# Swapping the two 48 KB weight regions between gate and up in an expert loop on one Trainium2 core

## The reference, cut to what matters

```python
def swiglu(h, wg, wu, wd):
    return (jax.nn.silu(h @ wg) * (h @ wu)) @ wd

def moe_swiglu(h, w_router, wg, wu, wd):
    logits = (t @ w_router).astype(jnp.float32)
    top_vals, top_idx = lax.top_k(logits, TOP_K)
    ...
    def expert(acc, xs):
        g_e, wg_e, wu_e, wd_e = xs
        return acc + g_e[:, None].astype(t.dtype) * swiglu(t, wg_e, wu_e, wd_e), None
```

## Time and profile before

| what | us |
|---|---|
| median of 3 runs (1561.59 to 1564.09) | 1562.27 |
| the profiled execution, its device time | 1563.21 |
| its span from the first to the last instruction | 1561.4 |
| start of item 0 on PE | about 643 |
| end of item 0 (big) on PE | 755.5 |
| end of item 1 (small) on PE | 858.6 |
| end of item 7 on PE | 1513.7 |

### The profile page before, as it was taken

The page is one execution under the profiler, slowest core; times in us unless marked ns, Lnnn a source line. Parts: engine busy times, 40 slices in busy tenths (PEclk is TensorE's granted clock), DMA queues, the critical chain, the costliest instruction groups (busy, mean ns, idle before and its releaser), DMA issues.

```text
span 1561.4 us, 26124 instructions
## 1 busy us (share of the span) xinstructions
PE 1453.6 (93%) x11620; PEld 854.2 (55%) x11620; DVE 486.5 (31%) x619; ACT 392.1 (25%) x457; POOL 73.1 (5%) x100
## 2 busy tenths in 40 slices
PE   9999999999999999999978999878999789997767
PEld 7888888888888788435322245232354222352225
DVE  7876654544666866400000010000000000000014
ACT  6665543434456554300000000000000000000003
POOL 0100000000000100210100000000001000001000
PEclk9999999999999999999999999999999999999998
DMA  9544555555274355978999999999999999999981
GB/s 332 191 153 147 175 201 188 188 189 188 86 272 164 136 195 224 385 299 342 370 410 424 414 412 412 405 412 415 419 415 379 412 426 414 409 411 398 422 347 50
DMA packets 101124, 477.46 MB, mean 306 GB/s; under 512 B 9084, under 2 KB 14364, under 8 KB 76444
## 3 DMA queue, kind: packets, MB, share of 16 engines
q1 hardware_dynamic: 96236, 465.93, 76.3%
q0 software_dynamic: 4608, 9.67, 2.3%
q10 hardware_dynamic: 176, 0.27, 0.1%
HBM read 469.13 MB, written 6.57 MB: 305 GB/s over the span
## 4 chain that ended last, share of the span: by engine, by line
PE 68%; DMA 25%; SPq 3%; DVE 2%; issue 1%; ACT 1%; ACTq 0%; DVEq 0%
PE ps L1747 30%; PE ps L1735 11%; PE ps L1737 11%; PE ps L1736 11%; DMA raw<-in_w_moe_gate 10%; DMA raw<-in_w_moe_down 5%; DMA whole<-in_w_moe_up 4%; DMA arena<-in_w_moe_down 3%; SPq L568 2%; DMA arena<-in_w_ple_gate 2%; PE ps L1744 1%; PE ps L1742 1%; PE ps L1743 1%; PE ps L1750 1%; PE ps L2195 1%
## 5 line engine op out<-in xcount | busy, mean ns | idle before, releaser
L1747 PE MATMUL ps<-whole,arena 128*32 128x256 f32 (+4 forms) x3136 | 329.0, 483 | 39.1 <-DMA whole<-in_w_moe_up 34.6
L1747 PE MATMUL ps<-raw,arena 128*32 128x256 f32 (+4 forms) x3136 | 324.3, 481 | 24.7 <-DMA raw<-in_w_moe_gate 13.7
L1087 DVE TENSOR_TENSOR w_lo<-raw,w_hi 128x2048 fp32r<-128x2048 f32 x99 | 226.1, 2290 | 124.9 <-ACT w_hi L745 124.6
L1735 PE MATMUL ps<-w_hi,hT_hi 128*128 128x512 f32 (+1 forms) x640 | 251.0, 392 | 3.6 <-DVE w_lo L1694 1.4
L1747 PEld LDWEIGHTS ps<-whole,arena 128*32 128x32 f32 (+1 forms) x3136 | 121.7, 116 | 236.6 <-issue 134.1
L1736 PE MATMUL ps<-w_lo,hT_hi 128*128 128x512 f32 (+1 forms) x640 | 246.7, 385 | 0.0
L1737 PE MATMUL ps<-w_hi,hT_lo 128*128 128x512 f32 (+1 forms) x640 | 246.7, 385 | 0.0
L1747 PEld LDWEIGHTS ps<-raw,arena 128*32 128x32 f32 (+1 forms) x3136 | 122.6, 115 | 220.7 <-issue 131.0
L1586 DVE TENSOR_TENSOR arena<-arena,ps 128x1536 f32<-128x1536 f32 (+3 forms) x16 | 21.1, 1321 | 646.8 <-PE ps L1747 646.8
L745 ACT ACTIVATE w_hi<-raw 128x2048 fp32r<-128x2048 f32 x99 | 189.3, 1914 | 110.8 <-PE ps L1737 105.5
L1747 PE MATMUL ps<-arena 128*32 128x32 f32 (+7 forms) x2056 | 151.8, 373 | 30.8 <-DMA arena<-in_w_moe_down 14.3
(11 more groups left out here) (314 smaller groups left out, 882.8 us busy)
## 6 DMA issues: line engine op xcount, KB each, us to landing
raw<-in_w_moe_gate SPq DMA_DIRECT2D x48, 1024.0 KB, 11.4
whole<-in_w_moe_up SPq DMA_DIRECT2D x48, 1024.0 KB, 20.9
raw<-in_w_moe_gate SPq DMA_DIRECT2D x64, 768.0 KB, 25.0
whole<-in_w_moe_up SPq DMA_DIRECT2D x64, 768.0 KB, 22.3
whole<-in_w_moe_down SPq DMA_DIRECT2D x24, 2048.0 KB, 16.3
raw<-in_w_moe_down SPq DMA_DIRECT2D x32, 1536.0 KB, 24.1
raw<-in_w_in SPq DMA_DIRECT2D x37, 1024.0 KB, 6.6
arena<-in_w_moe_gate SPq DMA_DIRECT2D x16, 1024.0 KB, 27.8
```

Of the source, the lines that this page charges most:

```text
L1087: nc.vector.tensor_tensor(w_lo[:, n % SLOTS, :], raw[:, raw_at(n), :], w_hi[:, n % SLOTS, :].bitcast(F32), ALU.subtract).then_inc(low_read ...
L1735: nc.tensor.matmul(o, x_parts[0][x_cols], parts[0], start=first, stop=False)
L1747: return nc.tensor.matmul(o, lhsT, rhs, start=start, stop=stop, skip_group_check=second_in_bank)
```

## The change

Gate and up swap their large regions. gate0.2 to gate0.7 and gate1 go to `whole_mem`; up0.0 to up0.5 and up1 go to `raw_mem`. `small_mem`, and the places of down0 and down1, stay. With that each piece waits for another piece than before:

| piece | waits for the use of, before | waits for the use of, after |
|---|---|---|
| gate0.0, gate0.1 (item t+1) | down0.0 (item t) | the same |
| gate0.2 to gate0.7 (item t+1) | down1.0, .1, .1, .2, .3, .3 (item t) | down0.1, .1, .2, .2, .3, .3 (item t) |
| up0.0 to up0.5 (item t+1) | down0.1, .1, .2, .2, .3, .3 (item t) | down1.0, .1, .1, .2, .3, .3 (item t) |
| up0.6, up0.7 | gate0.0, gate0.1 | the same |
| gate1.k | gate0.2 to gate0.7 | the same |
| up1.k | up0.k | up0.0, .1, .2, .2, .3, .4, .5, .5 |
| down0.0 | up0.7 | the same |
| down0.1, .2, .3 | up1.2, up1.5, up1.7 | gate1.2, gate1.5, gate1.7 |
| down1.0, .1, .2, .3 | gate1.2, .3, .5, .7 | up1.1, .3, .5, .7 |

In item 0 the large region that comes free first is `raw_mem`. So the six pieces that are issued under `low_ready` are now up0.0 to up0.5, and the six behind `units_used` are gate0.2 to gate0.7; both stand in the order of the queue as written. The landing semaphores are dealt out anew, 18 in place of 17. PE's, VectorE's, ScalarE's and GpSimd's streams keep their order. The core of the diff:

```diff
-    BEHIND_BEFORE = {GATE0 + k: DOWN0 if k < 2 else DOWN1 + (8 * (k - 2) + 7) // 12 for k in range(KD)}
-    BEHIND_BEFORE.update({UP0 + k: DOWN0 + 1 + k // 2 for k in range(6)})
-    BEHIND = {UP0 + k: GATE0 + k - 6 for k in (6, 7)}
+    HALF_ITEM = KD * 2
+    BEHIND_BEFORE = {GATE0: DOWN0, GATE0 + 1: DOWN0}
+    BEHIND_BEFORE.update({GATE0 + 2 + k: DOWN0 + 1 + k // 2 for k in range(6)})
+    BEHIND_BEFORE.update({UP0 + k: DOWN1 + (8 * k + 7) // 12 for k in range(6)})
+    BEHIND = {UP0 + 6: GATE0, UP0 + 7: GATE0 + 1, DOWN0: UP0 + 7}
     BEHIND.update({GATE1 + k: GATE0 + 2 + (6 * k + 5) // 8 for k in range(KD)})
-    BEHIND.update({UP_1 + k: UP0 + k for k in range(KD)})
-    BEHIND.update({DOWN0: UP0 + 7, DOWN0 + 1: UP_1 + 2, DOWN0 + 2: UP_1 + 5, DOWN0 + 3: UP_1 + 7})
-    BEHIND.update({DOWN1: GATE1 + 2, DOWN1 + 1: GATE1 + 3, DOWN1 + 2: GATE1 + 5, DOWN1 + 3: GATE1 + 7})
+    BEHIND.update({UP_1 + k: UP0 + (6 * k + 5) // 8 for k in range(KD)})
+    BEHIND.update({DOWN0 + 1 + u: GATE1 + (16 * u + 15) // 6 for u in range(3)})
+    BEHIND.update({DOWN1 + u: UP_1 + 2 * u + 1 for u in range(QUARTERS)})
...
         def in_piece(s, of_up, k):
             if s:
-                return (whole_mem if of_up else raw_mem)[:, k * WIDTHS[1]:(k + 1) * WIDTHS[1]]
+                return (raw_mem if of_up else whole_mem)[:, k * WIDTHS[1]:(k + 1) * WIDTHS[1]]
             if of_up:
-                return whole_mem[:, k * UNIT:(k + 1) * UNIT] if k < 6 else small_mem[:, (k - 6) * UNIT:(k - 5) * UNIT]
-            return small_mem[:, k * UNIT:(k + 1) * UNIT] if k < 2 else raw_mem[:, (k - 2) * UNIT:(k - 1) * UNIT]
+                return raw_mem[:, k * UNIT:(k + 1) * UNIT] if k < 6 else small_mem[:, (k - 6) * UNIT:(k - 5) * UNIT]
+            return small_mem[:, k * UNIT:(k + 1) * UNIT] if k < 2 else whole_mem[:, (k - 2) * UNIT:(k - 1) * UNIT]
...
-            for n, source in enumerate(expert_pieces(w_moe_gate[0, 0], w_moe_up[0, 0], w_moe_down[0, 0])):
-                if GATE0 + 2 <= n < UP0:
-                    sp.wait_ge(low_ready, UP1 - RAW_SLOTS + n - GATE0 - 1)
-                elif n == UP0:
-                    sp.wait_ge(units_used, UP1)
-                elif n in BEHIND:
-                    sp.wait_ge(pieces_used, BEHIND[n] + 1)
-                load_expert(n, source)
+            first = expert_pieces(w_moe_gate[0, 0], w_moe_up[0, 0], w_moe_down[0, 0])
+            load_expert(GATE0, first[GATE0])
+            load_expert(GATE0 + 1, first[GATE0 + 1])
+            for k in range(RAW_SLOTS):
+                sp.wait_ge(low_ready, UP1 - RAW_SLOTS + k + 1)
+                load_expert(UP0 + k, first[UP0 + k])
+            sp.wait_ge(units_used, UP1)
+            for k in range(2, KD):
+                load_expert(GATE0 + k, first[GATE0 + k])
+            for n in range(UP0 + 6, ITEM_PIECES):
+                sp.wait_ge(pieces_used, BEHIND[n] + 1)
+                load_expert(n, first[n])
```

More of the change, by code:

```diff
@@ L169, in build_trunk @@
-    BEHIND.update({DOWN0: UP0 + 7, DOWN0 + 1: UP_1 + 2, DOWN0 + 2: UP_1 + 5, DOWN0 + 3: UP_1 + 7})
-    BEHIND.update({DOWN1: GATE1 + 2, DOWN1 + 1: GATE1 + 3, DOWN1 + 2: GATE1 + 5, DOWN1 + 3: GATE1 + 7})
-    FILLED_BY = {n: (n // KD % 2 * KD + n % KD, n // (2 * KD)) for n in range(DOWN0)}
-    FILLED_BY.update({DOWN0: (2 * KD, 0), DOWN0 + 1: (KD, 2), DOWN0 + 2: (KD + 3, 2), DOWN0 + 3: (KD + 6, 2)})
-    FILLED_BY.update({DOWN1: (2, 2), DOWN1 + 1: (3, 2), DOWN1 + 2: (5, 2), DOWN1 + 3: (6, 2)})
@@ L175, in build_trunk @@
-    FILLS = [sum(by == spot for by, _ in FILLED_BY.values()) for spot in range(2 * KD + 1)]
+    HALF_ITEM = KD * 2
[3 more added lines that the diff above has]
+    BEHIND = {UP0 + 6: GATE0, UP0 + 7: GATE0 + 1, DOWN0: UP0 + 7}
+    BEHIND.update({GATE1 + k: GATE0 + 2 + (6 * k + 5) // 8 for k in range(KD)})
+    BEHIND.update({UP_1 + k: UP0 + (6 * k + 5) // 8 for k in range(KD)})
@@ new lines, in build_trunk @@
+    BEHIND.update({DOWN0 + 1 + u: GATE1 + (16 * u + 15) // 6 for u in range(3)})
+    BEHIND.update({DOWN1 + u: UP_1 + 2 * u + 1 for u in range(QUARTERS)})
+    ARENA_SPOT = HALF_ITEM
+    AFTER_FIRST = [0, 1, 2, 6, 3, 4, 5, 7]
+    FILLED_BY = {GATE0: (ARENA_SPOT, 0), GATE0 + 1: (ARENA_SPOT + 1, 0),
+                 UP0 + 6: (ARENA_SPOT, 1), UP0 + 7: (ARENA_SPOT + 1, 1), DOWN0: (ARENA_SPOT + 1, 2)}
+    FILLED_BY.update({GATE0 + 2 + k: (k, 0) for k in range(6)})
+    FILLED_BY.update({UP0 + k: (KD + k, 0) for k in range(6)})
@@ L177, in raw_at @@
+    FILLED_BY.update({GATE1 + k: (AFTER_FIRST[k], k not in (3, 7)) for k in range(KD)})
+    FILLED_BY.update({UP_1 + k: (KD + AFTER_FIRST[k], k not in (3, 7)) for k in range(KD)})
+    FILLED_BY.update({DOWN0 + 1: (2, 2), DOWN0 + 2: (4, 2), DOWN0 + 3: (5, 2)})
+    FILLED_BY.update({DOWN1: (KD + 1, 2), DOWN1 + 1: (KD + 2, 2), DOWN1 + 2: (KD + 4, 2), DOWN1 + 3: (KD + 5, 2)})
+    SPOTS = HALF_ITEM + 2
+    FILLS = [sum(by == spot for by, _ in FILLED_BY.values()) for spot in range(SPOTS)]
     def raw_at(n):
@@ L388, in build_trunk @@
         p_loaded = sem("p_loaded")
-        spot_filled = [sem(f"spot{n}_filled") for n in range(2 * KD + 1)]
+        spot_filled = [sem(f"spot{n}_filled") for n in range(SPOTS)]
         end_filled = [sem(f"end{n}_filled") for n in range(2)]
```

## The result

The changed kernel takes 1547.2 us (median of 4 runs, 1546.10 to 1548.41) against 1562.36 us of the kernel before beside it (1561.59 to 1564.09). The ratio is 0.990, with a 95% interval of 0.9885 to 0.9919: faster by 15.2 us.

A forecast was written before the change was run, and what follows sets the result against it. Transfers bound the kernel from item 1 on, so six pieces of 2.49 us sooner give 14.9 us; other terms cost zero. Median 1562.27 - 14.9 = 1547.4 us, range 1543.8 to 1551.0.

The forecast's parts named there:

- The bound and the hole: From item 1 transfers set the time at 412 GB/s; only the empty queue in item 0, 690 to 707 us, costs any.
- Event for event: At item 0's end, the down1 uses that released gate0.2 to gate0.7 of item 1 release up0.0 to up0.5, six pieces further.
- the end of item 0 decides: How far filling the 690 to 707 us hole helps is settled when item 0 ends, at 755.5 us.
- The size: Everything after item 0 comes 14.9 us sooner, with bounds of 12.4 and 17.6 us.
- Six pieces at the measured pace: In the saturated queue from item 1 on: 6 x 2.49 = 14.9 us gained.
- the bound of 17.6: Upper gain, 14.9 + 2.7 us, if the writes of item 0's results slip in where they cost nothing.
- No backlog at the events: Near item 0's end the queue is free in time: up0.4 could land at 760.7, ahead of 763.4 us.
- PE can give the time: In item 1, which took 103.2 us, PE could give 22 us where 14.9 are asked.
- The 81 us for PE's least time: Estimate of PE's shortest time for a small item with nothing late, including about 4 us for transposes.
- The cost of item 0's late gate: gate0.2 to gate0.7 of item 0, now issued behind `units_used`, cost zero, with 17.6 us of margin at the first.
- the slower rival: Item 0's gate is late: costs beyond 17.6 us of delay, outweighs the gain above 32.5, 1570 us at 40; chance 0.03.
- the landing at 630.4: In item 0 the piece in this place landed then with router traffic present, cited against a late gate.

The follow-up runs named there:

- The fourth experiment: Changed kernel with the new waits only from item 0 to item 1, items 2 to 7 waiting as before the change: 1547.66 us, ratio 0.9909.
- the changed kernel's second profile: The changed kernel unaltered, run once more beside the kernel before: 1546.96 us, ratio 0.9900, 15.9 us below before.
- the late gate0 alone: Changed kernel, but gate0.2 to gate0.7 of each next item wait for down1 as before the change; down0 keeps its early waits: 1561.98 us, ratio 0.9999.
- the three held-back kernels: Changed kernel with item 0's gate0.2 to gate0.7 held until logits turned, rows gathered, or gate0.1 used: 1549.62, 1553.82 and 1556.70 us.
- the kernel held back by 15.8 us: Changed kernel, but item 0's gate0.2 to gate0.7 are held until PE has gathered item 0's rows: 1553.82 us, ratio 0.9935.
- the kernel held back by 23.3 us: Changed kernel, but item 0's gate0.2 to gate0.7 are held until PE has used gate0.1: 1556.70 us, ratio 0.9957.

## Why the prediction was right, and where it was not

**The bound and the hole: right.** The saturated stretch kept its rate, and the whole gain came from one stall in item 0. The fourth experiment shows this, since it changes nothing in later items. down0.1 was issued at 690.54, forecast near 690.5. The rate from 690 to 707 was 348 GB/s, and 356 in the changed kernel's second profile, where over 350 was forecast.

**Event for event: right, and tested.** The six times of down1's use now release up0.0 to up0.5. The piece released at the end of item 0 was issued at 756.1 and landed 7.1 us later:

```profile
L578 SPq DMA_DIRECT2D raw<-in_w_moe_up x1: 332/332/332, 756.1 to 756.1; - x1
...
DMA to landing us min/median/max: 7.1/7.1/7.1
```

It landed at 763.2 where the prediction said 763.4. That the end of item 0 decides is shown by the late gate0 alone: the hole of 17 us was gone there, and no time was won.

**The size: 15.2 and 15.9 us in two comparisons for 14.9.** Six pieces at the measured pace carry it, and the rest lies inside the bound of 17.6. The end of item 1 moved by 16.4 us, more than the 14.9 at which I took it (842.2, forecast near 843.8). The pace of the six pieces is what was too small: between the landings behind 755 it is not 2.49 but 3.1 to 3.2 us for three pieces, in the time in which item 0's results are written, and before the change those were gate0.7 to up0.1, ahead of up0.4. up0.4 landed at 780.5 before and at 763.15 after, 17.3 us sooner. I had named this case as a bound and not taken it. The writes did not come free either: after the change it is up0.5 to up0.7 that take 3.0 to 3.2 us each, behind up0.4, and at up1.7 of item 1 16.4 us of the 17.3 are left. Why more than the 14.9 are left stays open.

**No backlog at the events: wrong by one piece, and it was luck that it cost nothing.** I let gate0.6 land on an idle queue at 745.1, but gate0.5 landed only at 745.05. From there each landing came one piece later than I had it: gate0.6 at 747.5, gate0.7 at 750.1, up0.0 at 752.6, up0.3 at 760.4 in place of 758.2. I gave the queue 2.7 us to spare at up0.4, 760.7 against 763.4. It had none: up0.4 landed at 763.15, 2.8 us behind up0.3, so that queue and event came out together. The forecast came out only because the two met; in the three held-back kernels the queue is the later one, and up0.4 lands later by it.

**PE can give the time: right.** PE passed gate0 and up0 in 1.72 us a piece, and first met the stream in up1. Neither ScalarE nor VectorE holds it up in item 1. The 81 us for PE's least time was not tested by itself.

**The cost of item 0's late gate: wrong in its rule.** "It costs nothing up to 17.6 us of delay" was worked out from PE's need of one piece, with the landing time of a quiet moment. The runs gave 2.7 us for 6.5 us of delay, 6.6 for 15.8 and 9.5 for 23.3. The step left out the queue: every transfer behind the held ones is late as well, and from 690 to 755 item 0 has only about 4 us of air for that. The forecast did not rest on it, for the change delays nothing there: its first held piece was issued at 625.80 and landed at 630.85, and before it was 625.37 and 630.4. But the point from which the slower rival would decide, 32.5 us, was not a measured one and should not be trusted. Nor did the landing at 630.4 speak against this rival: in the kernel before the stores are issued only from 636.7 on.

## What to carry to other kernels

Where a saturated queue follows a stage that is bound by something else, ask how many pieces are on chip or under way at the moment the bound changes; the difference in that count times the pace was the gain here, and stalls earlier in the stage counted only through it. The bytes moved up to that moment, read from one window, gave the same. Room for a ring is as large as its tightest pair of uses: to move one of two tight waits can be worth next to nothing, and the test is to move each alone. Margin for a held transfer has to be counted on the queue, for all that stands behind it, and not on the consumer of the first piece.

## What the runs showed that I had not expected

Stores of 3 MB from another queue lengthened the time from issue to landing from 5.0 to 8.9 us (issue at 625.4 and at 641.6), and it was 5.1 us again for the piece issued at 649.05, behind the stores. In the kernel before two landings among these stores came 3.5 and 3.9 us after the one ahead (637.8, 641.4, 645.2), in place of 2.49.

A short wait of PE cost nearly as much again in clock. In the kernel held back by 15.8 us PE waited 2.0 us up to 650.5, and then its granted clock was the lower of its two levels, 1.2 GHz, over this window, and back at 1.00 from 656 us on:

```profile
651.50:654.00 2.50, 2.50 (x16) 0.64 (x12) 0.00 (x0) 0.00 (x0) 2.13 (x4) 0.50 1.01 426
```

The six pieces behind the wait took 17.35 us in place of 15.63, so that a wait of 2.0 us made the end of item 0 3.8 us later. Behind the wait of 5.3 us in the kernel held back by 23.3 us they took 17.09: the longer wait cost no more clock than the shorter one.
